# Expert blocks of 64 rows, row transfers over all 128 partitions, norm rows by matrix product, and 8 KB pieces of the down weights

## The reference

```python
def hier_moe(x, w_group, w_expert, w_gate, w_up, w_down):      # 4 groups of 8 experts, top 2
    ...
    def expert_block(args):
        xb, e = args
        hmid = jax.nn.silu(xb @ w_gate[e]) * (xb @ w_up[e])    # 1024 -> 512
        return hmid @ w_down[e]                                # 512 -> 1024
    ...
for i in range(DEPTH):
    yp, state = mixer_i(xp)
    xp = layer_norm(ALPHA * xp + yp, ln1_g[i], ln1_b[i])
    mp = hier_moe(xp, ...)
    xp = layer_norm(ALPHA * xp + mp, ln2_g[i], ln2_b[i])
```

## Time and profile before

| what | value |
|---|---|
| median of three runs | 1586.69 us (1586.02 to 1588.08) |
| the profiled execution, its own time | 1591.29 us |
| its span, from the first to the last instruction | 1589.5 us |
| PE busy (matmul) | 1313.1 us, 83% |
| DVE busy | 411.0 us, 26% |
| ACT busy | 196.3 us, 12% |
| POOL busy | 189.1 us, 12% |
| mean granted clock of PE | 0.951 |
| read from HBM, written | 459.53 MB, 23.06 MB |

### The profile page before, as it was taken

The page is one execution under the profiler, slowest core; times in us unless marked ns, Lnnn a source line. Parts: engine busy times, 40 slices in busy tenths (PEclk is TensorE's granted clock), DMA queues, the critical chain, the costliest instruction groups (busy, mean ns, idle before and its releaser), DMA issues.

```text
span 1589.5 us, 19751 instructions
## 1 busy us (share of the span) xinstructions
PE 1313.1 (83%) x8238; PEld 886.6 (56%) x8238; DVE 411.0 (26%) x836; ACT 196.3 (12%) x313; POOL 189.1 (12%) x221
## 2 busy tenths in 40 slices
PE   7999998999877777778669999889977878787771
PEld 6888876666444444444258887656544444444430
DVE  1211114431111111111255663444111111111117
ACT  1000012000000000000044552200000000000001
POOL 0000000122111111111010000012211111111101
PEclk8999998899999999999879999989999999999995
DMA  9952204699999999999795112459999999999983
GB/s 234 330 192 106 106 1 160 239 400 399 408 405 413 404 404 409 400 402 413 234 306 207 56 51 108 160 209 374 402 395 404 407 402 403 399 407 394 412 296 107
DMA packets 111116, 475.23 MB, mean 299 GB/s; under 512 B 14332, under 2 KB 49148, under 8 KB 93637
## 3 DMA queue, kind: packets, MB, share of 16 engines
q1 hardware_dynamic: 95469, 447.35, 73.4%
q0 software_dynamic: 10048, 16.85, 3.1%
q10 hardware_dynamic: 5552, 10.39, 2.3%
HBM read 459.53 MB, written 23.06 MB: 304 GB/s over the span
## 4 chain that ended last, share of the span: by engine, by line
PE 42%; DMA 32%; SPq 18%; DVE 4%; issue 2%; ACT 2%; POOL 1%; ACTq 0%; POOLq 0%; DVEq 0%
PE ps L560 18%; SPq L367 18%; DMA ring<-in_moe_w_gate 15%; PE ps L798 9%; DMA ring<-in_moe_w_up 8%; PE ps L644 7%; DMA ring<-in_moe_w_down 4%; PE ps L819 4%; DMA ring<-yrows 2%; DMA ring<-in_a_w_in 1%; PE ps L788 1%; PE ps L662 1%; PE ps L696 1%; DMA yrows<-A,Bt 1%; DVE C L1522 1%
## 5 line engine op out<-in xcount | busy, mean ns | idle before, releaser
L798 PE MATMUL ps<-ring,A 128*64 128x256 f32 x4096 | 488.0, 394 | 142.2 <-DMA ring<-in_moe_w_up 92.4
L798 PEld LDWEIGHTS ps<-ring,A 128*64 128x64 f32 x4096 | 319.9, 142 | 328.5 <-issue 130.8
L560 PE MATMUL ps<-A,ring 128*128 128x260 f32 x1280 | 286.8, 387 | 2.6 <-DMA ring<-in_a_w_in 2.6
L819 PE MATMUL ps<-ring,C 128*64 128x512 f32 x1024 | 236.8, 603 | 41.4 <-DMA ring<-in_moe_w_down 17.0
L560 PEld LDWEIGHTS ps<-A,ring 128*128 128x128 f32 x1280 | 246.1, 193 | 41.4 <-issue 2.9
L1445 DVE TENSOR_TENSOR C<-C,ps 128x256 f32<-128x256 f32 x64 | 26.9, 420 | 753.9 <-ACT C L1063 753.9
L819 PEld LDWEIGHTS ps<-ring,C 128*64 128x64 f32 x1024 | 78.0, 138 | 159.0 <-issue 136.1
L499 POOL DMA_INDIRECT A<-x,idx x64 | 61.2, 956 | 491.2 <-PE ps L788 451.0
L644 PE MATMUL ps<-Bt,ring 128*128 128x260 f32 x512 | 116.1, 385 | 1.0 <-ACT C L986 0.8
L644 PEld LDWEIGHTS ps<-Bt,ring 128*128 128x128 f32 x512 | 96.1, 190 | 20.1 <-issue 2.1
L1063 ACT ACTIVATE C<-ps 128x256 f32<-128x256 f32 x64 | 24.5, 383 | 570.0 <-PE ps L798 570.0
(11 more groups left out here) (213 smaller groups left out, 674.9 us busy)
## 6 DMA issues: line engine op xcount, KB each, us to landing
ring<-in_moe_w_gate SPq DMA_DIRECT2D x64, 2048.0 KB, 39.9
ring<-in_moe_w_up SPq DMA_DIRECT2D x64, 2048.0 KB, 33.3
ring<-in_moe_w_down SPq DMA_DIRECT2D x64, 2048.0 KB, 36.9
ring<-in_a_w_in SPq DMA_DIRECT2D x24, 512.0 KB, 7.5
ring<-yrows SPq DMA_DIRECT2D x10, 832.0 KB
ring<-in_b_w_in SPq DMA_DIRECT2D x8, 1024.0 KB, 11.9
yrows<-C SPq DMA_DIRECT2D x5, 832.0 KB
x<-C ACTq DMA_DIRECT2D x10, 416.0 KB
```

The source lines that it names most:

```text
L560: mm = pe.matmul(bank, lhs(k), rhs(k), start=(k == 0), stop=(k == KT - 1))
L798: mm = pe.matmul(ps[hf * ROWS:(hf + 1) * ROWS, 1, u * FH:(u + 1) * FH], xgT[:, k, :], ring[:, slot, col:col + FH], start=(k == 0), stop=(k ...
L819: mm = pe.matmul(ps[nh * ROWS:(nh + 1) * ROWS, 2, :], hidT[:, at:at + ROWS], ring[:, slot, m * D + nh * 512:m * D + (nh + 1) * 512], start ...
```

## The change

- CAP becomes 64. The 64 places of an expert are no longer filled in order of rank: `slotno` gives place j the rank that it takes. For the gather the places 0 to 31 stand in partitions 0 to 31 and 32 to 63 in partitions 64 to 95, and the DMA has 128 rows, of which at least 64 (partitions 32 to 63 and 96 to 127) are always skipped. The product that makes `idx` is done in two halves.
- `turn_rows` takes the 128 partitions and is a matrix product with `placed`, a 128 x 64 part of the identity, in place of transposes of 64 partitions.
- The scatter is one indirect DMA of 128 partitions instead of two of 48; the sums for the destinations are made twice, once for each half of the partitions.
- `rows_back` and four of the five loads of the prompt take 128 rows (24 more than are used); `yrows` is 24 rows longer.
- Gain and shift come from `feat`, where they stand as columns, by 16 products with the identity (`spread_norm`) and four copies on ACT (`norm_rows`), in place of the loads. In each layer this stands after expert 1 and `turn_end`; for the last norm it stands after expert 30 of layer 1. All five tiles' `residual` move behind expert 2, without the extra multiplication of `shift`.
- The down weights are laid into the slot as two pieces of 8 KB a partition (four of 4 KB before), and the hidden values are turned with a stride to match.

```diff
-CAP = 48
+CAP = ROWS
+Q = ROWS // 2
...
-        picks = [[ring[:TT, ring_slot(POS_EXP[l] + 3 * (END - 1) + i // 2), (i % 2) * 2 * D:(i % 2 + 1) * 2 * D]
...
+        pick_rows = [[ring[:, ring_slot(POS_EXP[l] + 3 * (END - 1) + i // 2), (i % 2) * 2 * D:(i % 2 + 1) * 2 * D]
...
-        xg = [A[:ROWS, i * D:(i + 1) * D] for i in range(UNROLL)]
+        xg = [A[:, i * D:(i + 1) * D] for i in range(UNROLL)]
+        placed = ident[:, :].rearrange("p (h u q) -> p h u q", h=2, u=2)[:, :, 0, :]
...
-        downs = [a["moe_w_down"][l].rearrange("e (m p) n -> e p m n", p=P) for l in L]
+        downs = [a["moe_w_down"][l].rearrange("e (h p k) n -> e p h (k n)", h=2, k=2) for l in L]
...
-                    sp.dma_start(picks[l][i], rows_dram[i * TT:(i + 1) * TT]).then_inc(rows_in_sb[i], 16)
+                    sp.dma_start(pick_rows[l][i], rows_dram[i * TT:i * TT + P]).then_inc(rows_in_sb[i], 16)
...
-                sp.dma_start(xtok[:, i, :], a["x_prompt"][0, i * TT:(i + 1) * TT, :]).then_inc(x_in[i], 16)
+                sp.dma_start(xfull[:, i, :], a["x_prompt"][0, i * TT:i * TT + P, :]).then_inc(x_in[i], 16)
...
+            pool.iota(slotno[:, :], pattern=[[1, 2], [2, 8], [16, 4]], base=0, channel_multiplier=0,
+                      allow_small_or_imprecise_dtypes=True).then_inc(consts, 1)
+            pool.memset(idx[:, :], NOROW).then_inc(consts, 1)
...
-                        out=xg[e % UNROLL][:CAP], out_offset=None, in_=x1_dram[l],
+                        out=xg[e % UNROLL], out_offset=None, in_=x1_dram[l],
...
-                    for nh in range(2):
-                        pool.indirect_dma_start(
-                            out=half_rows, out_offset=bass.IndirectOffsetOnAxis(ap=where(nh), axis=0),
-                            in_=rows[nh * ROWS:nh * ROWS + CAP, :], in_offset=None,
-                            bounds_check=2 * TOPK * T - 1, oob_is_err=False,
-                        ).then_inc(done, 16)
+                    pool.indirect_dma_start(
+                        out=half_rows, out_offset=bass.IndirectOffsetOnAxis(ap=where, axis=0),
+                        in_=rows, in_offset=None, bounds_check=2 * TOPK * T - 1, oob_is_err=False,
+                    ).then_inc(done, 16)
...
-                        mm = pe.transpose(ps[:, 0, k * ROWS:(k + 1) * ROWS], xv[:, k, :], ident[:ROWS, :ROWS])
+                        mm = pe.matmul(ps[:, 0, k * ROWS:(k + 1) * ROWS].rearrange("p (h q) -> p h q", h=2), xv[:, k, :],
+                                       placed, start=True, stop=True)
...
+                def spread_norm(g, b):
+                    for r, bank in ((g, (6, 7)), (b, (3, 5))):
+                        for k in range(KT):
+                            mm = pe.matmul(ps[:TT, bank[k // 4], (k % 4) * P:(k % 4 + 1) * P],
+                                           feat[:, k, r:r + 1].broadcast_to([P, TT]), ident[:, :], start=True, stop=True)
+                        mm.then_inc(bc_mm, 1)
...
                     if e == 1:
                         turn_end()
+                        pe.wait_ge(endT_ok, l + 1)
+                        spread_norm(R_G1 + l, R_B1 + l)
...
+                    if l == 1 and e == TAIL[0]:
+                        pe.wait_ge(scaled, l + 1)
+                        spread_norm(R_G2 + l, R_B2 + l)
...
-                def norm_loads(q):
-
-                    g, b = (a["ln1_g"], a["ln1_b"]) if q % 2 == 0 else (a["ln2_g"], a["ln2_b"])
-                    act.dma_start(gain, g[l:l + 1, :].broadcast_to([TT, D])).then_inc(par_in, 16)
-                    act.dma_start(shift, b[l:l + 1, :].broadcast_to([TT, D])).then_inc(par_in, 16)
+                def norm_rows(q, scale):
+
+                    for v, (out, bank) in enumerate(((gain, (6, 7)), (shift, (3, 5)))):
+                        act.wait_ge(bc_mm, 2 * q + v + 1)
+                        for h in range(2):
+                            ins = act.activation(out[:, h * 512:(h + 1) * 512], ps[:TT, bank[h], :], ACT.Copy, scale=scale)
+                    ins.then_inc(bc_ok, 1)
...
-                tt(rowhot, over10(v10(1), CAP), iota[:, :CAP].unsqueeze(1).broadcast_to([TT, TOPK * NT, CAP]),
+                tt(rowhot, over10(v10(1), ROWS), slotno[:, :].unsqueeze(1).broadcast_to([TT, TOPK * NT, ROWS]),
```

More of the change, by code:

```diff
@@ L100, in rows_target @@
 def rows_target(l, j, n):
-    return 32 * (l * len(range(j, END, UNROLL)) + n)
+    return 16 * (l * len(range(j, END, UNROLL)) + n)
 def build(nc, a, outs):
@@ L144, in build @@
         wts = sb("wts", [TT, TOPK * NT])
[L145 to L146 removed]
+        idx = sb("idx", [P, NBLK], I32)
+        cur = sb("cur", [P, 2], I32)
+        dest_base = sb("dest_base", [P, 1])
         over_i = sb("over_i", [1, OVER + 1], I32)
@@ L167, in build @@
         gain, shift = Bt[:TT, 0:D], Bt[:TT, D:2 * D]
-        picks = [[ring[:TT, ring_slot(POS_EXP[l] + 3 * (END - 1) + i // 2), (i % 2) * 2 * D:(i % 2 + 1) * 2 * D]
-                  .rearrange("t (k d) -> t k d", k=TOPK) for i in range(NT)] for l in range(DEPTH)]
+        pick_rows = [[ring[:, ring_slot(POS_EXP[l] + 3 * (END - 1) + i // 2), (i % 2) * 2 * D:(i % 2 + 1) * 2 * D]
+                      .rearrange("t (k d) -> t k d", k=TOPK) for i in range(NT)] for l in range(DEPTH)]
+        picks = [[r[:TT] for r in rows] for rows in pick_rows]
         zeros = C[:TT, 5 * D + 256:5 * D + 768]
@@ L365, in expert @@
                     s = ring_slot(pos + u)
-                    out = ring[:, s, :] if u < 2 else ring[:, s, :].rearrange("p (m n) -> p m n", m=FT)
+                    out = ring[:, s, :] if u < 2 else ring[:, s, :].rearrange("p (h n) -> p h n", h=2)
                     sp.dma_start(out, w[l][e]).then_inc(loaded[s], 16)
@@ L1082, in _ @@
                     expert(e, e)
+                    if l == 1 and e == TAIL[0]:
+                        norm_rows(DEPTH, 1.0)
                 act.wait_ge(idx_ok[l], 2)
@@ L1150, in _ @@
             tt, stt = dve.tensor_tensor, dve.scalar_tensor_tensor
+            for nh in range(2):
+                dve.memset(dest_base[nh * ROWS:(nh + 1) * ROWS, :], float(NODEST + nh)).then_inc(consts, 1)
             for n_, i in enumerate(FIRST_ORDER):
@@ L1382, in _ @@
                 dve.wait_ge(idx_mm, 3 * l + 1)
-                tsc(idx[:, :NE], ps[:CAP, 5, :NE], float(NOROW), ALU.add).then_inc(idx_ok[l], 1)
+                for h in range(2):
+                    b = slice(h * ROWS, h * ROWS + Q)
+                    ins = tsc(idx[b, :NE], ps[b, 5, :NE], float(NOROW), ALU.add)
+                ins.then_inc(idx_ok[l], 1)
                 for k in range(TOPK):
@@ L1483, in _ @@
                     if e == 1:
-                        dve.wait_ge(par_in, 32 * (l + 1))
+                        end_turned()
+                    if e == 2:
+                        dve.wait_ge(bc_ok, l + 1)
                         dve.wait_ge(x1_out, 16 * NT * (l + 1))
-                        step(tsc(shift, shift, ALPHA, ALU.mult))
-                        for i in range(2):
-                            residual(i)
-                    if e == 2:
-                        end_turned()
-                        for i in range(2, NT):
+                        for i in range(NT):
                             ins = residual(i)
```

121 lines of the change are left out of this document (62 added, 59 removed).

## The result

The changed kernel takes 1699.72 us, median of 4 runs (1699.42 to 1700.92), where the kernel before has 1586.83 us beside it: ratio 1.0712, 95% interval 1.0694 to 1.0731, **slower by 7.1%**. The prediction said 1569 us, faster; the range ended at 1588.

The account below looks back on a forecast made before the run. Experts were taken as bound by the 16 DMA engines, the rest by PE. Start -3, layer 0 -6.7 and layer 1 -7.7 gave -17.4 us: 1586.7 to 1569 us, 8-in-10 range 1554 to 1588.

Parts of the forecast that it names:

- the price of `turn_rows`: PE's turn in each expert: 16 records of 120 ns, 1.9 us instead of 1.09, +0.8 us an expert.
- PE's spare 2 us: In the experts' stream PE was said to have some 2 us an expert to spare, hiding the longer turn.
- PE becomes the bound: Rival: turns at 224 ns a record make an expert 15.0 us against DMA's 14.8; 1586 us, chance 0.08.
- +13 (each turn and sum at twice its price): Upper bound on the cost at a layer's head, forecast at +8.9 us in layer 0, +7.6 in layer 1.
- Even places: Ends of each layer's stream: dealing ranks evenly fills all DMA engines, -7 us a layer.
- 8 KB pieces: Down weights in the stream: fewer, larger pieces, -2.7 us a layer, 5.4 in all; bounds 0 and 8.
- Skipped rows: Gather and scatter: 7104 more skipped rows at 10 ns, 4.4 us, +2.2 a layer; slower than before at 49 ns.
- Norm loads: Layer heads: removing the gain and shift loads frees the DMA stream, -3.4 us in layer 0, -6.8 in layer 1.
- The head of layer 0: PE's added work before the stream delays experts 1 and 2 by 6 and 12 us; +8.9 us.
- The start: Kernel's beginning: the prompt's rows load on 16 engines, -3 us; bounds 0 and -5.
- Rows back: Layer ends: tiles land before DVE needs them, no wait for `yrows` in layer 0; -4.7 us, layer 1 -1.0.
- PE's waits for weights vanish in the stream: Named sign in the changed profile that would show the prediction wrong; waits for gate and up were expected to remain.

Follow-up runs that it names:

- e13b: e7 with every product of turn_rows done twice (32 contiguous records); 1590.95 us, ratio 1.0027 to the kernel before.
- e7: The changed kernel, whole computation kept, with x1 stored in turned order so that turn_rows reads neighbouring elements; 1536.95 us, ratio 0.9675.
- e8: e7 with the ranks given to the places in order instead of evenly; 1549.19 us, ratio 0.9751.
- e4: The kernel before with only the 8 KB pieces of down and the strided hidden transposes they need; 1581.86 us, ratio 0.9956.
- e10: e7 with down in 4 KB pieces again and the hidden transposes read in order; 1544.72 us, ratio 0.9719.
- e11: e7 with the norm gain and shift loaded by DMA again and no spread_norm; 1531.83 us, ratio 0.9635.
- e6: The changed kernel with the gather into 64 partitions and turn_rows as 8 transposes reading neighbours (features in another order); 1571.67 us, ratio 0.9895.
- e3: The changed kernel with turn_rows reading 128 neighbouring elements instead of every eighth (features in another order); 1530.43 us, ratio 0.9630.
- e2: The kernel before with only the 8 transposes of turn_rows made products of 64 rows with the identity; 1689.18 us, ratio 1.0626.

## Why the prediction was wrong

**The step that failed** is the price of `turn_rows`: "16 records of 120 ns = 1.9 us, +0.8 us an expert. In the stream this lies in PE's spare 2 us." The number of records was right. The 120 ns came from a strided transpose; a product pays 242 ns for the same strided load, so the turn is 4.0 us, +2.9. That alone makes an expert 12.5 + 2.9 = 15.4 us against the DMA engines' 15. The 15 was a little low: from the down of expert 0 to that of expert 31 (298.90 to 777.52 us in layer 0) the kernel before takes 15.4 us an expert. So the longer turn alone uses up the spare time and the gain of the rest, and costs little against the kernel before; e13b shows it, with 15.2 us an expert and 1.0027. What makes the changed kernel slower was in no term: the strided loads bring 1.2 GHz to the down behind them, +1.7 us, and the expert is 17 us. The runs part the two: from the changed kernel (1.0712) to e13b (1.0027), which has as long a turn without the stride, 109 us go, and L838 and L798 shrink by 336.4 - 240.9 + 257.2 - 242.0 = 111 us of busy time. The rest of the way to e7 (0.9675), 56 us, is the length of the turn.

**The rival "PE becomes the bound"** was the right mechanism, with a chance of 0.08 and a price of 12 us back. It took 224 ns from a contiguous product's whole record and left the clock at 1. An expert 0.2 us over the DMA's pace looked harmless; at 2 us over it costs 2 x 58. The bound "+13 (each turn and sum at twice its price)" was applied to the head alone; the same doubling in the stream is what happened.

**Point by point, on the kernels without the stride.**
- *Even places*, -14: near, -12 (e8), though a share of 0.73 is left at the end of layer 1.
- *8 KB pieces*, -5.4: -7 in both kernels (e4, e10), the same within their intervals.
- *Skipped rows*, +4.4: not priced by a run of its own. From 560 to 760 us the indirect queue of e7 has 2435 packets at 3.9%, where the earlier trace rows has 1874 at 4.1%: nothing to be seen of 49 ns a row. Over the whole kernel the queue has 14176 packets instead of 10048, at 3.1% in both. The 8,000 more that were foreseen are 4,100, so packets and rows do not correspond one for one.
- *Norm loads*, -10.2, against `spread_norm`: the exchange costs 6 us (e11) instead of bringing some. The products stand on PE's path at the head: in layer 0 `project` of expert 2 starts 18.9 us after that of expert 1 in e7, 14.2 in e11.
- *The head of layer 0*: in the changed kernel experts 1 and 2 start at 308.14 and 330.78, against 303.71 and 317.10, with the first gather 4 us earlier: 8.5 and 17.7 us later relative to it, where 6 and 12 were foreseen. In e7 (301.22 and 320.15) it is 1.5 and 7.0. The destinations took 4.80 us (foreseen 6.4), `spread_norm` 3.74 (3.5), the two turns 8.1 instead of 3.8 (all in the changed kernel).
- *The start*, -3: in the changed kernel the first gather is issued at 273.49 instead of 277.54, 4 us earlier, though `idx` was priced at +1.4 ahead of it.
- *Rows back*: DVE waits nowhere for `yrows` in e7 (14.0 us before), as foreseen, and its last down waits for no DMA.
- *Not in the prediction*: a gather into the lower partitions slows the weights under way; over 128 partitions it doesn't. Worth (0.9895 - 0.9630) x 1586.7 = 42 us between e6 and e3.

With the turn at its foreseen price (2.0 us, e7) the time is 1537, not 1569: places and pieces came out near their sizes, the exchange of the norm loads worse, and the 42 us were missing. That e7 lies below the forecast is therefore no merit of the sum. In the changed kernel none of it shows, since PE sets the pace: the whole change is even 14 us slower than the turn alone (1.0712 against 1.0626).

**The signs that were named**: "PE's waits for weights vanish in the stream" was the right test; they went from 136 us to none.

## What to carry to other kernels

Price an operation from a row with the same operand, stride and mode: a strided fp32 weight load cost a product twice what the transpose's row said, and the lower clock in the products behind it nearly as much again (1.7 us an expert beside the 2.1 by which the turn was mis-priced). When a margin of 2 us an iteration hides an edit, work out what twice the edit's price does to the stream, not only to the head. Of an indirect DMA look at the partitions that it writes and at the rate of everything beside it, not at its own bytes.

## What the runs showed of the hardware

- Weight loads of 128 columns in fp32, per record: 242 ns in a product and 120 ns in a transpose when reading every eighth element; 116 and 72 ns when reading neighbours. For the strided product 64 rows (e2) and 128 rows gave the same; the others were run at one height each.
- Sixteen strided loads of 242 ns ahead of a down brought 1.2 GHz to it nearly always (60 of 64 downs over 5 us instead of 3.65); with 32 contiguous ones of nearly the same total length (3.8 against 4.0 us) 4 of 64 were slow, at the heads of the layers, as in e7; with eight strided and eight contiguous ones 26 were.
- A gather of 64 places (32.5 filled on average, 4 KB a row) into partitions 0 to 63 took the DMA rate from about 425 down to 330 and 373 GB/s for some 4 us at an unchanged busy share; into partitions 0, 2, ..., 126, or over 128 partitions, it did not.
